# Scoring two pages of cached keys in one set of matmuls

## The chip, the cores and the metric

One core of one Trainium2 chip runs the whole program in a single launch. The metric is device time in microseconds (us), the median of several executions. The profile describes one further execution of the same program: its span is the time from its first instruction to its last, and its rows give start and duration of each instruction on five engines, TensorE (PE in the profile, its weight loads PEld), VectorE (DVE), ScalarE (ACT), GpSimd (POOL) and SyncE (SP), together with DMA transfers and the clock that TensorE was granted, as a share of its full speed (1.00).

## The reference

The program is one inference step of a one-layer decoder: a mixer that joins differential attention and a convolution branch, then cross-attention, then a feed-forward block, for a prompt of 1024 tokens and for 8 decode sequences of 4 new tokens each. All numbers are f32. The part that matters here is the differential attention of the decode sequences over cached keys that lie in pages:

```
k_past = cache_k[l, page_table].reshape(dec_b, past, N_ATT_HEADS, ATT_V_DIM)
q2 = q.reshape(B, T, H, 2, DIFF_HEAD_DIM)
s_past = einsum('bqhjd,bkhjd->bjhqk', q2, k_past.reshape(B, P, H, 2, DIFF_HEAD_DIM))
w = diff_weights(concat([s_past, s_new]), bias, lam)   # softmax1 - lam * softmax2
```

Each of the 8 sequences has 16 pages of 128 past tokens, with 4 heads of 128 channels. So there are 128 pages of 128x512 numbers (256 KB each), and for each page and head a product of 8 query rows (4 tokens, two maps) with 128 keys. The prompt's own causal differential attention is computed with the same formula in 32 steps, one for each head (4) and block of 128 queries (8).

## The kernel before

The kernel is written with an instruction list for each engine and semaphores between them, and nothing is reordered: what stands first on an engine runs first there. After the input projection comes an attention stage. It is a loop of 32 **slots**, numbered from 0 here, one for each head and query block of the prompt, the longest block (8 key blocks) first in every head and the shortest last. `attend` (line 2192) is TensorE's part of a slot: it issues the prompt's scores (`scores`, line 2039, the matmuls of line 2053), and then, for the previous slot, the turning of its weights (`turn_weights`, line 2057, in one group of up to four blocks, or in two groups when the previous slot had five blocks or more) and its product with the values (`values`, line 2071). Between these it calls `page(0)` to `page(7)`, so that every slot also carries eight pages of the decode sequences. In slots 0 to 15 these are the 128 key pages, in slots 16 to 31 the 128 value pages. Two key pages out of eight stand directly behind each other only at some places: nothing stands between pages 0 and 1, 3 and 4, 6 and 7 of most slots, the first group of turned weights stands between 1 and 2, the second group between 2 and 3, the values between 4 and 5.

The path of a key page n through slots 0 to 15:

- SyncE loads it from the cache into one of 16 page buffers (`PG`, line 556), as soon as page n-16 has been turned. A load reads its page number from `PT` first.
- TensorE turns its four heads into one of two PSUM banks, 6 and 7 (`turn_keys`, line 2079, four transposes recorded at line 1813, the line of the helper `turn`). It waits for page n-2 to have left that bank.
- ScalarE copies the bank to SBUF (`key_taken`, line 852, recorded at line 733), into `KTS[n % 3]`.
- TensorE multiplies the queries with it (`page_scores`, line 2089, matmuls of line 2099). `key_page(n)` turns page n and then scores page n-2, so the copy has the time of one page. Each of the four heads has its own 32 output rows of PSUM bank 5, and the queries, padded with zeros, are the stationary operand with 32 columns; the 128 turned keys are the moving operand. One f32 product of the program shows as two matmul records and two weight loads in the profile; a transpose shows as one of each.
- After 16 pages the bank holds a sequence's scores, four pages a row group, and VectorE copies it out (`scores_out`, line 1485). The first score of the next sequence waits for that copy (`s_taken`).

In the same slots VectorE adds the prompt's bias (L1333), takes maxima (L1335, L1337), does one tap of the convolution in most slots (four pairs of L1310 and L1313), and ends the slot with a reciprocal and the weights (L1342, L1345, L1348), for which it waits for the two exponentials of ScalarE (line 832). `turn_weights` waits for the weights. ScalarE's list has the eight copies of the key pages of a slot with the copies of turned weights, the two exponentials and the scaling of the previous slot's output (L733 with `QK`, L849) between them, in a fixed order. The first exponential stands behind the copy of the slot's page 3, the scaling behind that of page 4, the second exponential behind that of page 5.

Of the kernel before, what the change touches and what calls it, by code (L numbers as in the profile page):

```python
# [20 lines left out]
F32 = mybir.dt.float32  # L21
F32R = mybir.dt.float32r
I32 = mybir.dt.int32
# [5 lines left out]
P = 128  # L29
# [3 lines left out]
TS = DB * DS  # L33
# [6 lines left out]
PAGES = 16  # L40
# [59 lines left out]
def hymba_step(nc, io):  # L100
    ctx = ExitStack()
    with ctx:
        def sem(name):
            return ctx.enter_context(nc.semaphore(name))
# [4 lines left out]
        R1, R2A, R2B, R3 = base, base + 2 * XB, base + 3 * XB, base + 4 * XB  # L109
        RW = R3 + XB  # L110
        RC = RW + 32768
        TB4 = T * 4

        def at(name, shape, dt, off):
            return nc.alloc_sbuf_tensor_at(name, shape, dt, offset=off)
# [53 lines left out]
        GP = at("GP", [P, CT, CK - 1 + TP], F32, R2B)  # L169
        GS = at("GS", [P, CT, DB, CK - 1 + DS], F32, R2B + 16864)  # L170
        ST = [at(f"ST{i}", [P, T], F32, R2B + 21216 + TB4 * i) for i in range(2)]
        KNEW = at("KNEW", [TS, 512], F32, R2B + 21216 + 2 * TB4)
        VNEW = at("VNEW", [TS, 512], F32, R2B + 21216 + 2 * TB4 + 2048)
        VTOK = at("VTOK", [P, QT, 512], F32, R3)
        CY = at("CY", [P, CT, T], F32, R3 + 16384)
        PT = at("PT", [P, P], I32, R2B + 21216 + 2 * TB4)[64:65, :]
        OTHER = at("OTHER", [TS, DB], F32, RC + 1824 + 352)
        VS = at("VS", [P, NH, TS], F32, R3 + 33280)
        DEC = at("DEC", [P, NH, TS], F32, R3 + 33280)
# [3 lines left out]
        SD = at("SD", [P, 2, PAGES * P], F32, R1 + 32768)  # L183
        CNEW = at("CNEW", [P, CT, TS], F32, R1 + 36864)
        CTOK = at("CTOK", [TS, 2, 512], F32, R1 + 32768)
        KTS = [at(f"KTS{i}", [P, 512], F32, R1 + (49152, 51200, 65536)[i]) for i in range(3)]
        CYS = at("CYS", [TS, 512], F32, R1 + 49152)
        OB = at("OB", [P, 512], F32, R1 + 51200)
        PB = [at("PB0", [P, 2, TP], F32, R1 + 53248), at("PB1", [P, 2, TP], F32, R2B + 21216)]
# [1 line left out]
        QZB = at("QZB", [P, 2 * QG], F32, RW + 8192)  # L191
# [22 lines left out]
        PS = ctx.enter_context(nc.psum_tensor("PS", [P, 8, 512], F32))  # L214
# [39 lines left out]
        KV = 2 * QT  # L254
# [140 lines left out]
        k_taken = sem("k_taken")  # L395
# [85 lines left out]
        def _(sp):  # L481
# [37 lines left out]
            def load(dst, src, s=rows_in):  # L519
                sp.dma_start(dst, src).then_inc(s, 16)  # L520
# [13 lines left out]
            load(OTHER[:, :], io["other"])  # L534
            load(PT, io["page_table"].rearrange("b n -> (b n)").unsqueeze(0), pt_in)
            for a in range(2):
# [15 lines left out]
            def page_in(cache, b, j, slot):  # L552

                page = sp.value_load(PT[:, PAGES * b + j:PAGES * b + j + 1], min_val=0, max_val=n_pages - 1)
                src = cache[0].rearrange("n s h d -> n s (h d)")[ds(page, 1), :, :].rearrange("n s d -> (n s) d")
# [47 lines left out]
        def _(pool):  # L603
            def store(dst, src, s=outs):
                pool.dma_start(dst, src).then_inc(s, 16)
# [53 lines left out]
            pool.wait_ge(rows_taken, 2)  # L659
            store(io["k_sample"][0].rearrange("b t h d -> (b t) (h d)"), KNEW[:, :])  # L660
            store(io["v_sample"][0].rearrange("b t h d -> (b t) (h d)"), VNEW[:, :])
# [7 lines left out]
            for b in range(DB):  # L669
                for r in range(1, PAGES, 2):  # L670
                    if b:
                        pool.wait_ge(v_used, PAGES * (b - 1) + r + 1)
                    else:
                        pool.wait_ge(k_turned, PAGES * (DB - 1) + r + 1)
                    page = pool.value_load(PT[:, PAGES * b + r:PAGES * b + r + 1], min_val=0, max_val=n_pages - 1)
                    src = io["cache_v"][0].rearrange("n s h d -> n s (h d)")[ds(page, 1), :, :]
# [54 lines left out]
        def _(act):  # L731
            def copy(dst, src, **kw):
                return act.activation(dst, src, ACT.Copy, **kw)  # L733
# [68 lines left out]
            with act.Fori(0, NH // 2) as i:  # L802
                for s in range(2):
                    t = 8 + 2 * i + s
# [8 lines left out]
            with act.Fori(0, NH // 2) as i:  # L813
                for s in range(2):
                    t = 12 + 2 * i + s
# [35 lines left out]

            def key_taken(n):
                act.wait_ge(k_turned, n + 1)
                copy(KTS[n % 3][:, :], PS[:, 6 + n % 2, :]).then_inc(k_taken, 1)

            def new_rows_in(i):

                if i == 0:
                    act.wait_ge(rows_turned, 1)
                    copy(KNEW[:, :], PS[0:TS, 4, :]).then_inc(rows_taken, 1)  # L860
                if i == 1:
# [29 lines left out]
            for s, (h, qb) in enumerate(ORDER[:KV]):  # L891
                last = ORDER[s - 1] if s else None
                n = 8 * s
                key_taken(n)
                if s == 0:
                    new_rows_in(0)
                key_taken(n + 1)
                if s == 0:
                    new_rows_in(1)
                if last:  # L900
                    weights_taken(*last, 0)
                key_taken(n + 2)
                if s == 0:
                    new_rows_in(2)
                if last and len(groups(last[1])) > 1:
                    weights_taken(*last, 1)
                key_taken(n + 3)
                if s == 0:
                    new_rows_in(3)
                att_exp(h, qb, 0)  # L910
                key_taken(n + 4)
                if last:
                    att_take(*last)
                key_taken(n + 5)
                att_exp(h, qb, 1)
                softmax_step(s)
                key_taken(n + 6)
                key_taken(n + 7)
# [131 lines left out]
            for s in range(3 * KT):  # L1050
                t = TILE0["out"] + KT + s
# [756 lines left out]
        def _(pe):  # L1808
            pe.sem_inc(tile_done, AHEAD)

            def turn(dst, src):
                k = src.shape[0]
                return pe.transpose(dst, src, IDENT[0:k, 0:k])  # L1813
# [148 lines left out]
            for a in range(2):  # L1962
                x = pe.matmul(PS[:, a, :], ONES[0:1, :], GROW[:, 512 * a:512 * a + 512], start=True, stop=True)
# [24 lines left out]
            with pe.Fori(0, NH) as i:  # L1988
                for u in range(2):
# [3 lines left out]
                    for b in range(QT):  # L1993
                        x = turn(PS[:, 6 + b // 4, P * (b % 4):P * (b % 4) + P], ST[u][:, P * b:P * b + P])
# [84 lines left out]
            def turn_keys(n):  # L2079

                r = n % PAGES
                pe.wait_ge(pg_in[r // 2], 32 * (n // PAGES) + 32)
                if n >= 2:
                    pe.wait_ge(k_taken, n - 1)
                for h in range(NH):
                    x = turn(PS[:, 6 + n % 2, P * h:P * h + P], PG[:, r, P * h:P * h + P])
                x.then_inc(k_turned, 1)

            def page_scores(n):

                g, b4, j4 = n // (4 * PAGES), n % PAGES // 4, n % 4
                pe.wait_ge(k_taken, n + 1)
                if n == 0:
                    pe.wait_ge(qb_ok, 2 * NH)
                if n % PAGES == 0 and n:
                    pe.wait_ge(s_taken, n // PAGES)
                for h in range(NH):
                    own = QG * g + P * b4 + 32 * h
                    x = pe.matmul(PS[32 * h:32 * h + 32, 5, P * j4:P * j4 + P], QZB[:, own:own + 32],  # L2099
                                  KTS[n % 3][:, P * h:P * h + P], start=(n % PAGES == 0), stop=(n % PAGES == PAGES - 1),  # L2100
                                  skip_group_check=True)
                if n % PAGES == PAGES - 1:
                    x.then_inc(s_done, 1)

            def key_page(n):
                turn_keys(n)
                if n >= 2:
                    page_scores(n - 2)

            def turn_probs(g, c):  # L2110

# [132 lines left out]

            for s in range(KV):
                attend(s, lambda t: key_page(8 * s + t))
            for n in (8 * KV - 2, 8 * KV - 1):
                page_scores(n)
            for s in range(KV, NH * QT):
                attend(s, lambda t: value_page(8 * (s - KV) + t))  # L2250
            turn_weights(NH - 1, 0, 0)
# [3 lines left out]
            for h in range(NH):  # L2255
                x = pe.matmul(PS[:, 5, 0:SC].rearrange("p (g b h r) -> p g b h r", g=2, b=4, h=NH)[:, :, :, h, :],
                              VNEW[:, P * h:P * h + P],
                              SNEW[:, :].rearrange("p (g h b r) -> p g h b r", g=2, h=NH, b=4)[:, :, h, :, :],
                              start=True, stop=True)
# [20 lines left out]
            def part(k, c, first, last):  # L2280
                cols = slice(CHUNK * c, CHUNK * c + CHUNK)
                out = PS[:, c, 0:CHUNK]
                pe.matmul(out, WH[0][:, k, :], XH[:, k, cols], start=first, stop=False)
                pe.matmul(out, WH[0][:, k, :], XL[:, k, cols], start=False, stop=False)
                return pe.matmul(out, WL[0][:, k, :], XH[:, k, cols], start=False, stop=last)
# [23 lines left out]
            for c in (2, 3):  # L2309
                arrived(NH + 3 + c)  # L2310
                for n in range(2):
                    x = part(NH + c, n, False, c == 3)
# [123 lines left out]
            for q in range(QT + 1):  # L2436
# [12 lines left out]
                if q == QT:  # L2449
                    pe.wait_ge(xsm_v, 7)  # L2450
                    for a in range(2):
                        x = turn(PS[:, 2, P * a:P * a + P], OX[:, P * a:P * a + P])
# [8 lines left out]
                if q == 4:  # L2461
                    pe.wait_ge(xsm_v, 4)
                    for a in range(2):
                        x = turn(PS[:, 2, P * a:P * a + P], XS[:, P * a:P * a + P])
# [17 lines left out]
            def gate_step(u, c, k):  # L2482
                cols = slice(CHUNK * c, CHUNK * c + CHUNK)
                out = PS[:, 3 * u + c, 0:CHUNK]
                pe.matmul(out, WH[u][:, k, :], XH[:, k, cols], start=(k == 0), stop=False)
                pe.matmul(out, WH[u][:, k, :], XL[:, k, cols], start=False, stop=False)
                return pe.matmul(out, WL[u][:, k, :], XH[:, k, cols], start=False, stop=(k == KT - 1))
# [20 lines left out]
            for k in range(KT):  # L2508
                input_of("ffn", 1)(k)
                x = gate_step(0, 2, k)  # L2510
# [3 lines left out]
            for k in range(KT):  # L2514
                x = gate_step(1, 2, k)
# [77 lines left out]
```

## Time and profile before

| | us |
|---|---|
| runs of the kernel before | 1914.32, 1904.26, 1913.89 (median 1913.89) |
| profiled execution, time | 1911.54 |
| its span | 1910.0 |
| TensorE busy in the span | 1799.2 (94%) |
| VectorE, ScalarE busy | 940.7 (49%), 548.6 (29%) |
| transposes of key pages (L1813 with PG), busy | 82.0 |
| page scores (L2099), busy | 54.5 |
| copies of turned pages (L733 with KTS), busy | 75.7 |

The first page is turned at 283.9 us and the prompt's scores of slot 16 begin at 462.6 us, so the key pages take a tenth of the span. Busy is the union of the instructions' times on an engine. Matmuls overlap each other, so their mean duration (286 ns for a page score) is far more than the time that each adds; the start of the next work on the engine tells what a set of them costs.

### The profile page before, as it was taken

The page shows a single profiled execution, that of the slowest core. Times are in us where ns is not written, and L with a number is a line of the kernel's source. Part 1 is how long each engine was busy: PE and PEld are TensorE (multiplying, and loading weights), DVE is VectorE, ACT ScalarE, POOL GpSimd, SP SyncE. Part 2 cuts the span into 40 slices and gives each one's busy share as a digit, 9 for nine tenths or more (in the row PEclk, how much of TensorE's full clock was granted, in tenths as well). Part 3 has the DMA queues.
Part 4 walks back from the last instruction along what each step waited for, and adds up shares of the span by engine and source line. Part 5 has one row for each costly group of instructions (what it writes and reads, how often), then busy time and mean ns, then how long its engine had stood idle before and what let it go on. Part 6 is the DMA issues. An engine that isn't in the chain of part 4 may idle for free.

```text
span 1910.0 us, 33059 instructions
## 1 busy us (share of the span) xinstructions
PE 1799.2 (94%) x13461; PEld 1657.0 (87%) x13461; DVE 940.7 (49%) x1245; ACT 548.6 (29%) x993; POOL 91.6 (5%) x138
## 2 busy tenths in 40 slices
PE   7999998999988988998999899999999999999996
PEld 6999985665557978996789789999999999999995
DVE  6328887886665466222353753333233332233456
ACT  6202116676565255103432531110001000010133
POOL 2100010001320000001000000000000000000001
PEclk9999999999998999999999999999999999999997
DMA  5422127766884223234402331111112111111322
GB/s 173 137 71 77 55 69 223 226 186 199 286 284 182 67 89 133 89 110 155 150 30 80 94 114 44 44 44 45 44 54 56 45 44 45 44 44 38 134 74 91
DMA packets 149374, 199.06 MB, mean 104 GB/s; under 512 B 8105, under 2 KB 110715, under 8 KB 148872
## 3 DMA queue, kind: packets, MB, share of 16 engines
q1 hardware_dynamic: 134318, 133.00, 22.8%
q0 software_dynamic: 14944, 64.53, 9.6%
q8 instruction: 76, 1.25, 0.3%
q14 instruction: 34, 0.28, 0.0%
q10 hardware_dynamic: 2, 0.00, 0.0%
HBM read 177.19 MB, written 20.74 MB: 104 GB/s over the span
## 4 chain that ended last, share of the span: by engine, by line
PE 53%; DVE 5%; ACT 2%; issue 2%; POOLq 0%; POOL 0%; DVEq 0%; ACTq 0%
PE PS L1823 15%; PE PS L1824 15%; PE PS L1825 15%; PE PS L1813 2%; PE PS L2376 2%; PE PS L2397 1%; DVE WL L1550 1%; ACT WH L733 1%; PE PS L1837 1%; PE PS L1838 1%; PE PS L1839 1%; PE PS L1862 1%; DVE H L1580 1%; DVE Y L1577 1%; DVE HST L1778 0%
## 5 line engine op out<-in xcount | busy, mean ns | idle before, releaser
L1823 PE MATMUL PS<-XH,WH 128*128 128x352 f32 x1984 | 645.0, 325 | 7.7 <-DVE WL L1550 5.7
L1824 PE MATMUL PS<-XL,WH 128*128 128x352 f32 x1984 | 638.1, 322 | 0.0
L1825 PE MATMUL PS<-XH,WL 128*128 128x352 f32 x1984 | 637.6, 321 | 0.0
L1196 DVE CAST WH<-RAW 128x1024 fp32r<-128x1024 f32 x112 | 78.8, 704 | 634.2 <-PE PS L1825 614.0
L1823 PEld LDWEIGHTS PS<-XH,WH 128*128 128x128 f32 x1984 | 374.1, 189 | 9.6 <-DVE WL L1550 6.5
L1824 PEld LDWEIGHTS PS<-XL,WH 128*128 128x128 f32 x1984 | 374.7, 189 | 0.0
L1825 PEld LDWEIGHTS PS<-XH,WL 128*128 128x128 f32 x1984 | 373.6, 188 | 0.0
L1310 DVE SCALAR_TENSOR_TENSOR CY<-GP,DW,CY 128x1024 f32<-128x1024 f32 x124 | 158.5, 1278 | 1.0 <-DVE CY L1313 1.0
L1823 PE MATMUL PS<-HH,WH 128*128 128x352 f32 x468 | 154.0, 329 | 2.9 <-DVE Y L1769 2.7
L1824 PE MATMUL PS<-HL,WH 128*128 128x352 f32 x468 | 152.4, 326 | 0.0
L1825 PE MATMUL PS<-HH,WL 128*128 128x352 f32 x468 | 152.2, 325 | 0.0
L1198 DVE TENSOR_TENSOR WL<-RAW,WH 128x1024 fp32r<-128x1024 f32 x112 | 137.3, 1226 | 3.8
L1142 ACT ACTIVATE TA<-TA 128x1056 f32<-128x1056 f32 x22 | 23.9, 1087 | 364.9 <-DVE TA L1730 364.9
L733 ACT ACTIVATE HH<-TA 128x1056 f32 x22 | 23.9, 1086 | 251.9 <-DVE TA L1736 251.9
L1823 PEld LDWEIGHTS PS<-HH,WH 128*128 128x128 f32 x468 | 89.9, 192 | 3.7 <-DVE WL L1550 3.2
L1824 PEld LDWEIGHTS PS<-HL,WH 128*128 128x128 f32 x468 | 90.0, 192 | 0.0
L1825 PEld LDWEIGHTS PS<-HH,WL 128*128 128x128 f32 x468 | 89.7, 192 | 0.0
L1813 PE MATMUL PS<-IDENT,PG 128*128 128x128 f32 x512 | 82.0, 283 | 5.2 <-DMA PG<-in_cache_k 2.6
L733 ACT ACTIVATE KTS<-PS 128x512 f32<-128x512 f32 x128 | 75.7, 601 | 35.7 <-PE PS L1813 35.3
L1813 PEld LDWEIGHTS PS<-IDENT,PG 128*128 128x128 f32 x512 | 56.7, 142 | 25.5 <-issue 21.3
L1550 DVE TENSOR_TENSOR WL<-RAW,WH 128x1024 fp32r<-128x1024 f32 x38 | 46.5, 1223 | 58.7 <-ACT WH L733 58.7
L2099 PE MATMUL PS<-KTS,QZB 128*32 128x128 f32 x1024 | 54.5, 286 | 2.2 <-DVE SD L1485 2.0
(342 smaller groups left out, 2303.5 us busy)
## 6 DMA issues: line engine op xcount, KB each, us to landing
PG<-in_cache_k SPq DMA_DIRECT2D x128, 256.0 KB, 3.0
PG<-in_cache_v SPq DMA_DIRECT2D x64, 256.0 KB, 4.3
PG<-in_cache_v POOLq DMA_DIRECT2D x64, 256.0 KB, 4.4
RAW<-in_w_gate SPq DMA_DIRECT2D x22, 512.0 KB, 4.1
RAW<-in_w_up SPq DMA_DIRECT2D x22, 512.0 KB, 5.2
RAW<-in_w_in SPq DMA_DIRECT2D x20, 512.0 KB, 6.4
RAW<-in_w_out SPq DMA_DIRECT2D x16, 512.0 KB, 4.5
RAW<-in_w_xo SPq DMA_DIRECT2D x16, 512.0 KB, 4.3
```

The costliest lines, as they stand in the source:

```text
L733: return act.activation(dst, src, ACT.Copy, **kw)
L1142: act.activation(TA[:, :], TA[:, :], ACT.Silu).then_inc(silu_ok, 1)
L1196: dve.tensor_copy(WH[v % 2][:, :, :], raw).then_inc(hi_done, 1)
L1198: dve.tensor_tensor(WL[v % 2][:, :, :], raw, WH[v % 2][:, :, :].bitcast(F32), ALU.subtract)\
L1310: dve.scalar_tensor_tensor(out=CY[:, c, 0:TP], in0=GP[:, c, ds(j, TP)], scalar=w, in1=CY[:, c, 0:TP], op0=ALU.mult, op1=ALU.add).then_inc( ...
L1550: dve.tensor_tensor(WL[t % 2][:, :, :], RAW[t // 2 % 2][:, :, P * (t % 2):P * (t % 2) + P], WH[t % 2][:, :, :].bitcast(F32), ALU.subtract) ...
L1813: return pe.transpose(dst, src, IDENT[0:k, 0:k])
L1823: pe.matmul(out, WH[u][:, k, :], xh[:, k, cols], start=(k == 0), stop=False)
L1824: pe.matmul(out, WH[u][:, k, :], xl[:, k, cols], start=False, stop=False)
L1825: mm = pe.matmul(out, WL[u][:, k, :], xh[:, k, cols], start=False, stop=(k == kt - 1))
L2099: x = pe.matmul(PS[32 * h:32 * h + 32, 5, P * j4:P * j4 + P], QZB[:, own:own + 32], KTS[n % 3][:, P * h:P * h + P], start=(n % PAGES == 0) ...
L2376: x = pe.matmul(PSF[:, NMEM * h:NMEM * h + NMEM], Y[:, 2 * h + k, P * q:P * q + P], KMT[:, 2 * h + k, :], start=(k == 0), stop=(k == 1))
```

## The change

Key pages are scored in pairs. A key page is still turned and copied by itself, but on even pages `key_page` now only turns. On an odd page n it turns, and then `pair_scores(n - 3)` scores pages n-3 and n-2 with one set of matmuls, in which the moving operand has 256 columns: 128 of the first page and 128 of the second. The products, their sums and the bank they go to stay as they were; there are 256 products of the program instead of 512. The pair waits for both copies, and the wait for VectorE's copy of the previous sequence moves with the pair.

A pair needs its two turned pages in one tile, so three buffers `KTS[n % 3]` become two tiles of two pages each. The second page of the second tile lies where `KNEW` and the page table `PT` were, and these two move; they keep their size. The second tile's two pages are 65,504 bytes apart in each partition, the first tile's 2,048 bytes.

```diff
-        KNEW = at("KNEW", [TS, 512], F32, R2B + 21216 + 2 * TB4)
+        KNEW = at("KNEW", [TS, 512], F32, R1 + 40960)
...
-        PT = at("PT", [P, P], I32, R2B + 21216 + 2 * TB4)[64:65, :]
+        PT = at("PT", [P, P], I32, R2B + 21216 + 2 * TB4 + 2048)[64:65, :]
...
-        KTS = [at(f"KTS{i}", [P, 512], F32, R1 + (49152, 51200, 65536)[i]) for i in range(3)]
+        KTS_AT = (49152, 51200, 65536, R2B - R1 + 21216 + 2 * TB4)
+        KTS = [at(f"KTS{i}", [P, 2, (KTS_AT[2 * i + 1] - KTS_AT[2 * i]) // 4], F32, R1 + KTS_AT[2 * i]) for i in range(2)]
...
             def key_taken(n):
                 act.wait_ge(k_turned, n + 1)
-                copy(KTS[n % 3][:, :], PS[:, 6 + n % 2, :]).then_inc(k_taken, 1)
+                copy(KTS[n // 2 % 2][:, n % 2, 0:512], PS[:, 6 + n % 2, :]).then_inc(k_taken, 1)
...
-            def page_scores(n):
+            def pair_scores(n):
 
                 g, b4, j4 = n // (4 * PAGES), n % PAGES // 4, n % 4
-                pe.wait_ge(k_taken, n + 1)
+                pe.wait_ge(k_taken, n + 2)
                 if n == 0:
                     pe.wait_ge(qb_ok, 2 * NH)
                 if n % PAGES == 0 and n:
                     pe.wait_ge(s_taken, n // PAGES)
                 for h in range(NH):
                     own = QG * g + P * b4 + 32 * h
-                    x = pe.matmul(PS[32 * h:32 * h + 32, 5, P * j4:P * j4 + P], QZB[:, own:own + 32],
-                                  KTS[n % 3][:, P * h:P * h + P], start=(n % PAGES == 0), stop=(n % PAGES == PAGES - 1),
-                                  skip_group_check=True)
-                if n % PAGES == PAGES - 1:
+                    x = pe.matmul(PS[32 * h:32 * h + 32, 5, P * j4:P * j4 + 2 * P].rearrange("p (a t) -> p a t", a=2),
+                                  QZB[:, own:own + 32], KTS[n // 2 % 2][:, :, P * h:P * h + P],
+                                  start=(n % PAGES == 0), stop=(n % PAGES == PAGES - 2), skip_group_check=True)
+                if n % PAGES == PAGES - 2:
                     x.then_inc(s_done, 1)
 
             def key_page(n):
                 turn_keys(n)
-                if n >= 2:
-                    page_scores(n - 2)
+                if n % 2 and n >= 3:
+                    pair_scores(n - 3)
...
             for s in range(KV):
                 attend(s, lambda t: key_page(8 * s + t))
-            for n in (8 * KV - 2, 8 * KV - 1):
-                page_scores(n)
+            pair_scores(8 * KV - 2)
```

## Rows read from the trace of the kernel before

**Rows 1.** Busy time by window: stretch, us, PE, PEld, DVE, ACT, POOL, PEclk, DMA, GB/s.
```profile
285.00:465.00 180.00, 169.70 (x1886) 110.65 (x1887) 140.26 (x243) 121.82 (x273) 8.39 (x16) 0.99 0.71 210
...
356.20:365.50 9.30, 9.30 (x115) 6.00 (x111) 8.44 (x16) 6.54 (x17) 0.00 (x0) 1.00 0.80 229
```

**Rows 2.** Groups by form, 285 to 465 us: busy, mean ns, idle before and releaser.
```profile
L733 ACT ACTIVATE KTS<-PS 128x512 f32<-128x512 f32 x128 | 75.7, 601 | 35.7 <-PE PS L1813 35.3
...
L2099 PE MATMUL PS<-KTS,QZB 128*32 128x128 f32 x1024 | 54.5, 286 | 2.2 <-DVE SD L1485 2.0
```

**Rows 3.** Waits, 285 to 465 us: who waited for whom, total us, times, longest.
```profile
DVE SMALL L1342 <- ACT PB L832: 24.4, 13, 6.1
...
PEld PS L2099 <- ACT KTS L733: 7.9, 37, 1.6
...
PE PS L1813 <- ACT KTS L733: 2.6, 2, 1.6
...
PE PS L2099 <- DVE SD L1485: 2.0, 2, 1.4
...
PE PS L1813 <- DVE SNEW L1407: 1.1, 1, 1.1
```

**Rows 4.** Timeline of PE in slot 5: start, us, instruction; turns and scores alternate.
```profile
350.20 0.42 PE L2099 MATMUL PS<-KTS,QZB 128*32 128x128 f32 x8
350.56 0.66 PE L1813 MATMUL PS<-IDENT,PG 128*128 128x128 f32 x4
351.14 0.43 PE L2099 MATMUL PS<-KTS,QZB 128*32 128x128 f32 x8
351.50 0.65 PE L1813 MATMUL PS<-IDENT,PG 128*128 128x128 f32 x4
```

**Rows 5.** Timeline, slots 4 and 5: turns behind full-width work, and the second group of weights.
```profile
338.97 0.66 PE L1813 MATMUL PS<-IDENT,PB 128*128 128x128 f32 x4
...
339.47 0.60 PE L1813 MATMUL PS<-IDENT,PG 128*128 128x128 f32 x4
339.67 0.60 ACT L733 ACTIVATE WT<-PS 128x512 f32<-128x512 f32 x1 [0.34 <-PE PS L1813]
...
340.46 0.33 PE L1813 MATMUL PS<-IDENT,PB 128*128 128x128 f32 x1
...
353.44 0.60 PE L1813 MATMUL PS<-IDENT,PG 128*128 128x128 f32 x4
353.97 0.42 PE L2099 MATMUL PS<-KTS,QZB 128*32 128x128 f32 x8
```

**Rows 6.** Timeline of PE: prompt scores with 256 and with 128 moving columns, and what follows.
```profile
356.21 0.70 PE L2053 MATMUL PS<-QK 64*128 64x256 f32 x4
356.84 0.66 PE L1813 MATMUL PS<-IDENT,PG 128*128 128x128 f32 x4
...
365.48 0.49 PE L2053 MATMUL PS<-QK 64*128 64x128 f32 x4
365.91 0.66 PE L1813 MATMUL PS<-IDENT,PG 128*128 128x128 f32 x4
```

**Rows 7.** By form and timeline: the scores of the new tokens, a moving operand in pieces.
```profile
L2027 PE MATMUL PS<-QZB,QK 128*32 128x64 f32 x8 | 0.6, 219 | 0.0
...
291.54 0.61 PE L2027 MATMUL PS<-QZB,QK 128*32 128x64 f32 x8
```

**Rows 8.** Timeline of PE: the first turned weights of slot 1.
```profile
303.22 0.92 PE L1813 MATMUL PS<-IDENT,PB 128*128 128x128 f32 x4 [2.67 <-issue]
```

**Rows 9.** Timeline of SP in slot 5, and the page's DMA issues (KB each, us to landing).
```profile
349.80 12.40 SPq L556 DMA_DIRECT2D PG<-in_cache_k  x11
...
PG<-in_cache_k SPq DMA_DIRECT2D x128, 256.0 KB, 3.0
```

**Rows 10.** Timeline: VectorE's weights of slot 6, and TensorE's turn of them in slot 7.
```profile
365.36 0.48 DVE L1348 SCALAR_TENSOR_TENSOR PB<-PB,SMALL 128x256 f32<-128x256 f32 x1
...
367.79 0.44 PE L1813 MATMUL PS<-IDENT,PB 128*128 128x128 f32 x2
```

## The prediction

> **What bounds the kernel now.** I read the busy time of the stage first. From 285 to 465 us TensorE is busy 169.70 of 180 us, VectorE 140.26, ScalarE 121.82 [rows 1]. So TensorE sets the pace, but VectorE stands close behind: in slot 6 it is busy 8.44 of 9.30 us [rows 1]. The waits come next, to see how often TensorE is held up. What they name is small: 7.9 and 2.6 us for ScalarE's copies of turned pages, 2.0 us for VectorE's copy of a sequence's scores, 1.1 us for its copy behind SNEW [rows 3], and once 2.67 us for the first turned weights [rows 8]. The other side waits longer: VectorE waits 24.4 us in 13 places for the exponentials [rows 3], and ScalarE 35.7 us for turned pages [rows 2]. An edit that shortens TensorE's list therefore shortens the stage, until VectorE's spare time is used up. Third, the timeline of TensorE, because busy time hides what matters: the score records have a mean of 286 ns, yet 1024 of them take 54.5 us together [rows 2]. Only the distance from one start to the next shows what a set costs.
>
> **The change part by part: the sets.** A page's scores start at 350.20, its successor's turns at 350.56, the next scores at 351.14 [rows 4]. So a set of scores costs 0.36 us, a set of four turns behind it 0.58, and a page 0.94; two pages cost 1.88.
>
> After the change a pair is turns, turns, one wide set. Turns that follow full-width work are cheaper than turns that follow a score: from 353.44 to 353.97 is 0.53 us [rows 5], and four turns followed by four more take 339.47 - 338.97 = 0.50 [rows 5]. Two blocks of turns then cost 0.50 + 0.53 = 1.03. This holds wherever the page stands, since turned weights and values, the work between pages, are full-width too.
>
> The wide set isn't in the trace. Below, it costs 0.36, as if the columns were free; above, 2 x 0.36 = 0.72, as if nothing were shared. The nearest rows are the prompt's scores, also two f32 products side by side in a part of the array: with 128 columns such a set takes 365.91 - 365.48 = 0.43 us, with 256 it takes 356.84 - 356.21 = 0.63 [rows 6]. So 0.21 us of the set scales with 128 columns and the rest is paid once per set. I take 0.36 + 0.21 = 0.57.
>
> A pair then costs 1.03 + 0.57 = 1.60 instead of 1.88, a gain of 0.28, and 64 pairs gain 18 us. By the bounds of the wide set the gain is 0.13 to 0.49 a pair, 8 to 31 us. The part that goes isn't the multiplying, it is the passage from transposes to scores and back.
>
> **What of it stays.** From the 18 us I take what is caught by waits.
>
> Slots 0 and 1: the first weights at 303.22 wait 2.67 us for VectorE's chain [rows 8], which has work of its own for the new tokens. What TensorE gains before that (five pairs, 1.4 us) only lengthens that wait, except some 0.25 us by which ScalarE reaches the first exponential sooner. Loss 1.15.
>
> Slots 1 to 4 and 9 to 12 turn weights in two groups through the same bank, and the second waits for ScalarE's copy of the first. Today the scores of page 2 lie in between and hide it. The copy starts 0.70 us after the first group and takes 0.60, so the second group can't start before about 1.34; it started at 340.46, 1.49 behind 338.97 [rows 5]. After the change only a block of turns is between, ready at about 0.94. The new wait is 0.40; eight of them would be 3.2 us, of which I count 2.9, as the first falls in a delayed stretch.
>
> Waits that move: the wait of 2.0 us, in two places, is for the copy of the previous sequence's scores [rows 3]. The pair asks for it one page later. In slot 2 I expect it gone, a gain of 0.6; in slot 8 VectorE's chain is longer and the wait stays, but page 3's turns are then done before it, so the slot keeps its gain.
>
> VectorE and ScalarE: in slot 12 the turn of the decode weights waits 1.1 us for VectorE's copy behind SNEW [rows 3], and that copy stands after a convolution tap, so what TensorE gains earlier in the slot is lost: 0.45. The 2.6 us in which turns wait for copies are two waits, 1.6 in slot 0 and the other 1.0 at the start of slot 10 [rows 3]; there the copy stands behind ScalarE's decode exponential, so the 0.28 that TensorE gains after slot 9's second exponential is lost.
>
> Elsewhere the spare time suffices. In the slots from 5 to 7 TensorE gains 4 x 0.28 = 1.1 us each, and VectorE has 9.30 - 8.44 = 0.86 spare [rows 1], so it falls behind by about 0.3 us a slot, some 0.9 by slot 7. There it can afford more: its weights of slot 6 are done at 365.84 and turned at 367.79, 1.95 us later [rows 10]. Slot 8 has no convolution tap and it catches up.
>
> SyncE issues page loads 12.40/11 = 1.1 us apart and a load lands in 3.0 us [rows 9]. Eight pages are 9.0 us, more than the new slots 6 and 7 (9.3 - 1.1 = 8.2 us), but loads run up to 16 pages ahead, and over the 16 slots TensorE still needs more than 1.2 us a page. So this costs nothing; without the lead, a page of slots 5 to 8 would arrive about 1 us late in every slot. The move of KNEW and PT changes no instruction.
>
> The sum: 18.2 - 1.15 - 2.9 + 0.6 - 0.45 - 0.28 = 14.0 us. Behind slot 15 the same chain starts 14 us earlier, and nothing there hangs on an absolute time. The profiled execution took 1911.5 us (span 1910.0), so 1897.5. It lies 2.4 us under the median of the runs shown, which is 1913.9; profile and runs average 1911.0, so I take the profiled one as typical and predict 1898.
>
> **The rivals.** *All of it stays* (0.13): the second group's wait falls beside other delays and VectorE keeps up. Then 1911.5 - 18 = 1893.5. For it speaks VectorE's 24.4 us of waiting [rows 3], against it that this is spread unevenly (slot 15 alone has 6.1).
>
> *ScalarE's copies become the wait* (0.17). Two turned pages in a row fill both banks. A copy starts 0.70 us after the first turn of its block [rows 5] and takes 0.60 [rows 2]; the second of two starts when the first is done, so it ends at 0.70 + 1.20 = 1.90 after the pair's first turn. Its bank is wanted again after the pair and one more block of turns, at 1.60 + 0.50 = 2.10. That leaves 0.2. Between some copies stand exponentials and the output's scaling. If 0.3 us were missing at two places in each slot, 32 x 0.3 = 9.6 us would go and the gain shrink to 4: 1907. Against it: ScalarE waits 35.7 us for turned pages today [rows 2] and is busy 6.54 us of a slot of 9.30 [rows 1]. The Trainium skill, TensorEngine Tiling (Array Packing), section PSUM Bottleneck, warns of this case: splitting the array speeds up TensorE but not the copies out of PSUM, which may become the bottleneck. By that rule this rival would be the result; the trace has the copies at 75.7 us in a stage of 180 [rows 2].
>
> *The wide set costs nearly two narrow ones* (0.05), so that only the saved passage between turns remains: 8 us less the same losses of about 4, again 1907.
>
> *Slower* (0.06): the moving operand now comes in two pieces, in every second pair 65,504 bytes apart. If its second piece were streamed slowly, a wide set could exceed two narrow ones. To end 0.5% slower than before (1923.5) each pair must lose (14 + 9.6)/64 = 0.37 us, so the wide set must take 0.94 instead of 0.57; it decides from 0.79, where the gain of 14 is gone. Against it: eight score matmuls with 64 columns in pieces of 8 take 0.61 us in all, of which the last one's own 0.22, so 0.06 each [rows 7], no slower per column than the rest.
>
> **How the numbers follow.** The forecast, 10 to 17 us saved, has 0.59; the rivals 0.13, 0.17, 0.05 and 0.06. About 0.5%, 9.6 us, is what a measurement of this kernel can tell from no change. Faster by more takes the forecast and the first rival: 0.72. Within it fall the second and third: 0.22. Slower: 0.06. The forecast's own range is 1893 to 1904. The range to hold eight times in ten reaches from 1890 (the full gain, and 3 us for the difference between executions) to 1908 (the second and third rival).
>
> **What would show it.** In the profile after: 512 score records of 256 columns in place of 1024; a pair's period near 1.60 us where no wait is in it; 0.57 us from a wide set to the next turns; a wait of about 0.4 us of L1813 with PB for ScalarE's WT in slots 2 to 4 and 9 to 12; VectorE's waiting at L1342 much smaller than 24.4 us; slot 16 beginning near 448.6 instead of 462.6. The prediction is wrong if waits of L1813 with PG for KTS grow past 5 us, if 0.57 is nearer 0.72, or if slot 16 begins 14 us earlier and the end doesn't.

## The result, and the profile after

| | before | after |
|---|---|---|
| median of the runs, us | 1912.24 (8 runs, 1904.12 to 1914.32) | 1897.88 (8 runs, 1894.95 to 1900.11) |
| profiled execution, us | 1911.54 | 1897.24 |
| its span, us | 1910.0 | 1895.7 |

The ratio is 0.9926, with a 95% interval of 0.9915 to 0.9937: 14 us, or 0.7%, faster. The forecast was 1898.0. In the changed kernel all lines named here stand one lower (turns L1814, copies L734, scores L2100).

First the busy time by window (columns as in [rows 1]), of the key pages' stage and of the new slot 6, which now takes 8.00 us instead of 9.30.

```profile
285.00:451.00 166.00, 153.56 (x1395) 101.36 (x1393) 140.82 (x245) 119.03 (x273) 8.49 (x16) 0.99 0.75 228
350.60:358.60 8.00, 8.00 (x82) 5.35 (x78) 7.87 (x13) 6.41 (x17) 0.00 (x0) 1.00 0.79 242
```

TensorE's busy time in the stage fell by 16.1 us; VectorE's and ScalarE's busy times are nearly as before, in a shorter stage. In slot 6 VectorE is now busy 7.87 of 8.00 us: its idle time, 0.86 us of the slot before, has shrunk to 0.13. Next the groups by form of the same stage, beside [rows 2].

```profile
L734 ACT ACTIVATE KTS<-PS 128x512 f32<-128x512 f32 x128 | 72.4, 600 | 26.4 <-PE PS L1814 26.1
...
L2100 PE MATMUL PS<-KTS,QZB 128*32 128x256 f32 x512 | 40.9, 391 | 1.5 <-DVE SD L1486 1.3 <-ACT KTS L734 0.2
```

There are 512 records of 256 columns, and they are busy 40.9 us where 1024 narrow ones took 54.5. Then the waits of 285 to 451 us, beside [rows 3].

```profile
DVE SMALL L1343 <- ACT PB L833: 13.9, 6, 4.7
...
PEld PS L1814 <- ACT WT L734: 3.7, 8, 0.5
PE PS L1814 <- ACT KTS L734: 3.0, 2, 1.9
PEld PS L2100 <- ACT KTS L734: 2.7, 5, 1.5
...
PE PS L1814 <- ACT WT L734: 1.8, 7, 0.3
...
PE PS L1814 <- DVE SNEW L1408: 1.5, 1, 1.5
...
PE PS L2100 <- DVE SD L1486: 1.3, 1, 1.3
```

VectorE waits in 6 places instead of 13. TensorE's matmuls have one new wait, for WT, in seven places (slots 2 to 4 and 9 to 12): the second group of turned weights waits for ScalarE's copy of the first. The weight loads (PEld) show it in eight places, with slot 1; before, they had waited for WT in six places, 1.2 us in all, and the matmuls in none. Of the two waits for the scores' copy (SD) one is left, and the one behind SNEW grew from 1.1 to 1.5. Last the timeline of TensorE in slot 4, beside [rows 4, 5].

```profile
334.57 0.64 PE L2100 MATMUL PS<-KTS,QZB 128*32 128x256 f32 x8
335.14 0.66 PE L1814 MATMUL PS<-IDENT,PB 128*128 128x128 f32 x4
335.63 0.60 PE L1814 MATMUL PS<-IDENT,PG 128*128 128x128 f32 x4
336.49 0.33 PE L1814 MATMUL PS<-IDENT,PB 128*128 128x128 f32 x1 [0.25 <-ACT WT L734]
...
339.89 0.64 PE L2100 MATMUL PS<-KTS,QZB 128*32 128x256 f32 x8
340.46 1.09 PE L1814 MATMUL PS<-IDENT,PG 128*128 128x128 f32 x8
341.48 0.64 PE L2100 MATMUL PS<-KTS,QZB 128*32 128x256 f32 x8
```

A wide set costs 340.46 - 339.89 = 0.57 us, the two blocks of turns behind it 341.48 - 340.46 = 1.02, so a pair 1.59 instead of 1.88. The second group of weights starts 336.49 - 335.14 = 1.35 behind the first, and its row shows 0.25 of idle time. Before, it started 1.49 behind [rows 5], with the scores of a page in between.

Where the gain comes from is read from the first record of the prompt's scores in each slot (start of L2053 before, L2054 after):

| slot | before, us | after, us | earlier by | gained in the slot |
|---|---|---|---|---|
| 0 | 280.07 | 280.15 | -0.08 | 0.95 |
| 1 | 295.61 | 294.74 | 0.87 | 0.54 |
| 2 | 313.11 | 311.70 | 1.41 | 1.38 |
| 3 | 325.16 | 322.37 | 2.79 | 0.75 |
| 4 | 336.03 | 332.49 | 3.54 | 0.86 |
| 5 to 8 | 346.45 | 342.05 | 4.40 | 1.21, 1.27, 1.20, 1.24 |
| 9 | 385.63 | 376.31 | 9.32 | 0.74 |
| 10 | 397.58 | 387.52 | 10.06 | 0.63 |
| 11 | 410.01 | 399.32 | 10.69 | 0.74 |
| 12 | 420.87 | 409.44 | 11.43 | 0.30 |
| 13 to 15 | 432.86 | 421.13 | 11.73 | 1.20, 1.29, 1.10 |
| 16 | 462.63 | 447.31 | 15.32 | |

The gain is spread over the slots: about 1.2 us (four pairs of 0.30) where nothing interferes, 0.63 to 0.86 where weights are turned in two groups, 0.30 where the wait behind SNEW takes more. Slots 0 and 1 differ from execution to execution, so their gain is less sure than that of slots 2 to 15 (the last experiment has numbers). From slot 16 to the end 1.0 us is lost again; the last experiment bears on that too.

### The profile page after: what moved, and what is told of

Read it like the earlier page. It is cut to its first block, busy times and chain, and to the rows that moved or that the text cites. A ratio compares the mean times of both kernels' runs of the same rounds, so it can differ in the third digit from the quotient of the medians.

```text
span 1895.7 us, 32035 instructions
## 1 busy us (share of the span) xinstructions
PE 1785.1 (94%) x12949; PEld 1649.9 (87%) x12949; DVE 940.2 (50%) x1245; ACT 546.3 (29%) x993; POOL 92.1 (5%) x138
## 3 DMA queue, kind: packets, MB, share of 16 engines
q8 instruction: 72, 1.18, 0.3%
## 4 chain that ended last, share of the span: by engine, by line
PE 54%; DVE 5%; ACT 2%; issue 2%; POOLq 0%; POOL 0%; DVEq 0%; ACTq 0%
PE PS L1824 15%; PE PS L1825 15%; PE PS L1826 15%; PE PS L1814 2%; PE PS L2376 2%; PE PS L2397 1%; DVE WL L1551 1%; ACT WH L734 1%; PE PS L1838 1%; PE PS L1840 1%; PE PS L1839 1%; PE PS L1863 1%; DVE H L1581 1%; DVE Y L1578 1%; DVE HST L1779 0%
## 5 line engine op out<-in xcount | busy, mean ns | idle before, releaser
L734 ACT ACTIVATE HH<-TA 128x1056 f32 x22 | 23.9, 1088 | 251.9 <-DVE TA L1737 251.9
L734 ACT ACTIVATE KTS<-PS 128x512 f32<-128x512 f32 x128 | 72.4, 600 | 26.4 <-PE PS L1814 26.1
L1814 PE MATMUL PS<-IDENT,PG 128*128 128x128 f32 x512 | 74.2, 280 | 5.1 <-ACT KTS L734 3.0
L1814 PEld LDWEIGHTS PS<-IDENT,PG 128*128 128x128 f32 x512 | 57.3, 142 | 23.8 <-issue 19.9
L833 ACT ACTIVATE PB<-PS,SMALL 128x1024 f32<-128x1024 f32 (+7 forms) x64 | 47.7, 745 | 2.1 <-DVE SMALL L1338 2.0
```

Source lines behind the costliest of these rows:

```text
L833: act.activation(PB[r][:, m, 0:n], PSF[:, TP * m:TP * m + n], ACT.Exp, bias=NMX2[r][:, m:m + 1], scale=SCALE, accum_out=SUM2[r][:, m:m + 1 ...
```

## The experiments

The theory is the forecast's: the time lies in the passages between turns and scores, the new wait is the second group's, and TensorE still sets the pace. The rivals are that the wide set itself saves time, that the buffers do, and that VectorE or ScalarE limits the gain.

**Narrow sets in the order of the change.** Order and buffers are those of the change; only the pair is scored by two sets of 128 columns, one directly behind the other.

```diff
-                for h in range(NH):
-                    own = QG * g + P * b4 + 32 * h
-                    x = pe.matmul(PS[32 * h:32 * h + 32, 5, P * j4:P * j4 + 2 * P].rearrange("p (a t) -> p a t", a=2),
-                                  QZB[:, own:own + 32], KTS[n // 2 % 2][:, :, P * h:P * h + P],
...
+                for a in range(2):
+                    for h in range(NH):
+                        own = QG * g + P * b4 + 32 * h
+                        x = pe.matmul(PS[32 * h:32 * h + 32, 5, P * (j4 + a):P * (j4 + a) + P], QZB[:, own:own + 32],
+                                      KTS[n // 2 % 2][:, a, P * h:P * h + P], start=(n % PAGES + a == 0),
...
```

> The order, the waits and the buffers of the change stay, but a pair is scored by two sets of 128 columns, one behind the other, in place of one set of 256. Theory: most of the gain is the saved passage from transposes to scores and back, and little comes from the width. Three narrow sets that stood behind each other at the end of the key pages before the change began 0.24 us apart, and the wide set adds 0.21 us for its second page, so a pair should cost 0.03 us more than after the change: 64 x 0.03 = 2 us slower than the change, still 12 us faster than before. Rival, the width makes the gain (a set pays its fixed part again each time): a second set costs 0.36, a pair 0.15 us more, 10 us slower than the change, 5 us faster than before.

Measured: 1896.96 us (median of 6, 1894.55 to 1897.71), ratio to before 0.9921 (0.9905 to 0.9937). The interval covers that of the change. The timeline of TensorE in slot 4:

```profile
339.82 0.65 PE L2101 MATMUL PS<-KTS,QZB 128*32 128x128 f32 x16
340.40 1.09 PE L1814 MATMUL PS<-IDENT,PG 128*128 128x128 f32 x8
341.42 0.65 PE L2101 MATMUL PS<-KTS,QZB 128*32 128x128 f32 x16
```

Two narrow sets take 0.58 us together, one wide set 0.57. Between the starts of slots 2 and 16 this kernel needs 135.84 us, the change 135.61: the 256 columns are worth 0.23 us over 56 pairs, where 0.03 a pair, 1.7 us, had been expected. The loads of the stationary operand doubled (1024 records, busy 24.3 us instead of 10.1) and cost no more than that on the path. The row behind the 0.24 of the expectation stood in the trace of before: at the end of the key pages one narrow set begins at 461.52 and the next at 461.76. The third begins only at 462.28, behind a wait.

**The buffers of the change in the order of before.** The other half of that pair of kernels: two tiles of two pages, moved KNEW and PT, but each page is scored by itself behind the next but one's turns.

```diff
-                pe.wait_ge(k_taken, n + 2)
+                pe.wait_ge(k_taken, n + 1)
...
-                                  QZB[:, own:own + 32], KTS[n // 2 % 2][:, :, P * h:P * h + P],
...
+                    x = pe.matmul(PS[32 * h:32 * h + 32, 5, P * j4:P * j4 + P], QZB[:, own:own + 32],
+                                  KTS[n // 2 % 2][:, n % 2, P * h:P * h + P], start=(n % PAGES == 0),
...
-                if n % 2 and n >= 3:
-                    pair_scores(n - 3)
+                if n >= 2:
+                    page_scores(n - 2)
```

> The buffers of the change (four turned pages, KNEW and PT moved) with the order of before: each page's turns followed by the scores of the page two back, in sets of 128 columns. It differs from the run with narrow sets in order alone. Theory: the order is the gain, so this takes the time of before, within 1 us at slot 16, and lies 15 us behind the run with narrow sets there. Rival, the fourth buffer or the places of the buffers make part of the gain: 3 us or more faster than before.

Measured: 1910.53 us (median of 10, 1902.57 to 1913.92), ratio 0.999 (0.9972 to 1.0009): the interval holds 1, so no change is shown. Slot 16 begins at 460.94, 1.69 us earlier than before, where at most 1 was expected; but 1.68 of that is there at the start of slot 2 (311.43), and 1.08 at the start of slot 0. From slot 2 on the buffers alone give 0.01 us (149.51 us to slot 16, 149.52 before). The timeline in slot 4:

```profile
336.00 0.43 PE L2100 MATMUL PS<-KTS,QZB 128*32 128x128 f32 x8
336.35 0.66 PE L1814 MATMUL PS<-IDENT,PG 128*128 128x128 f32 x4
336.94 0.43 PE L2100 MATMUL PS<-KTS,QZB 128*32 128x128 f32 x8
```

The page costs 336.94 - 336.00 = 0.94, as before. This kernel and the one with narrow sets issue the same matmuls of the same shape on the same buffers and differ only in their order, and in the wait for the copies that goes with it; between slots 2 and 16 they need 149.51 and 135.84 us. So 13.67 of the 13.91 us that the change gains there are order: two blocks of turns and two sets of scores in a row instead of one and one. The difference lies in both: two sets fall from 2 x 0.35 = 0.70 to 0.58, two blocks of turns from 2 x 0.59 = 1.18 to 1.02. The Trainium skill, TensorEngine Tiling (Array Packing), section Key Properties, says that a change of the tiling mode drains TensorE. These rows agree in the sense that each pair with one passage to the 32-column scores and back instead of two is 1.88 - 1.60 = 0.28 us shorter; that the drain is the cause they don't show.

**A lighter VectorE.** In slots 1 to 15 two of the four channel groups of a convolution tap work on 64 columns instead of 1024. A part of the convolution is left out.

```diff
+                    m = 64 if light and c >= 2 else TP
-                    dve.scalar_tensor_tensor(out=CY[:, c, 0:TP], in0=GP[:, c, ds(j, TP)], scalar=w,
-                                             in1=CY[:, c, 0:TP], op0=ALU.mult, op1=ALU.add).then_inc(conv_step, 1)
+                    dve.scalar_tensor_tensor(out=CY[:, c, 0:m], in0=GP[:, c, ds(j, m)], scalar=w,
+                                             in1=CY[:, c, 0:m], op0=ALU.mult, op1=ALU.add).then_inc(conv_step, 1)
...
-                    conv(tap)
+                    conv(tap, True)
```

> The change, with VectorE's convolution tap in slots 1 to 15 cut to 64 of 1024 columns for two of the four channel groups (that part of the convolution is left out), about 2.3 us less of VectorE's work in a slot. Theory: TensorE sets the pace and VectorE's lag is affordable, so slot 16 begins earlier by only some 1.5 to 2 us, the wait behind SNEW in slot 12 that the tap causes. Rival, VectorE became the second bound after the change: slot 16 begins 5 us or more earlier, with gains in slots 5 to 7, 10 and 11.

Measured, in one execution: 1896.84 us; slot 16 begins 1.87 us earlier than after the change (445.44), as expected. The waits of 285 to 450 us show that VectorE really became free:

```profile
DVE SMALL L1344 <- ACT PB L833: 34.7, 16, 5.3
```

It now waits for the exponentials in 16 places, and yet TensorE starts slot 12 only 0.29 us earlier. The other 1.59 us come in slot 12 alone, where the wait behind SNEW is gone. So VectorE, busy 7.87 of 8.00 us in slot 6, does not set the pace of the plain slots; it costs time in one place, where a copy for TensorE stands behind a tap.

**The second group of weights later.** In slots that turn weights in two groups, page 3 is turned first, then the second group, then the pair is scored; ScalarE takes page 3 before the second group's copy.

```diff
+                key_taken(n + 3)
                 if last and len(groups(last[1])) > 1:
                     weights_taken(*last, 1)
...
-                key_taken(n + 3)
...
-                if last and len(groups(last[1])) > 1:
-                    turn_weights(*last, 1)
-                page(3)
+                two = last and len(groups(last[1])) > 1
+                if two and s < KV:
+                    turn_keys(8 * s + 3)
+                    turn_weights(*last, 1)
+                    pair_scores(8 * s)
+                else:
+                    if two:
+                        turn_weights(*last, 1)
+                    page(3)
```

> The change, with the second group of turned weights moved behind the turns of page 3 and ahead of the scores (ScalarE's copies in the same order). Theory: the wait of 0.25 us in seven slots for ScalarE's copy of the first group goes and comes back nowhere, 1.8 us faster than the change, 16 us faster than before. Rival: it turns into a wait of the values for the second group's copy, and the time stays that of the change.

Measured: 1892.73 us (median of 6, 1889.52 to 1896.36), ratio 0.9907 (0.9891 to 0.9924). The timeline of TensorE in slot 4:

```profile
332.22 0.66 PE L1814 MATMUL PS<-IDENT,PB 128*128 128x128 f32 x4
332.71 1.04 PE L1814 MATMUL PS<-IDENT,PG 128*128 128x128 f32 x8
333.58 0.31 PE L1814 MATMUL PS<-IDENT,PB 128*128 128x128 f32 x1
333.82 0.42 PE L2100 MATMUL PS<-KTS,QZB 128*32 128x256 f32 x4
```

The second group now starts 1.36 behind the first, as after the change (1.35), but two blocks of turns lie between instead of one, and no idle time is left. These rows also show where the time of a passage lies: a block of turns with other turns on both sides takes (333.58 - 332.71)/2 = 0.435 us, one between two sets of scores 0.59. Slots 3 and 4 are each 0.43 us shorter than after the change, slots 9 to 11 0.43 to 0.44. So the new wait cost 0.43 in each of these five, close to the forecast's 0.40, and not the 0.25 that stands in the row: of a wait the row shows the time in which no matmul was running, and the tail of the matmuls before it hides the rest. The gain of 4.36 us at the start of slot 16 is not all the edit's, since slot 0 began 1.57 earlier in this execution, slot 1 0.18 later and slot 2 2.19 earlier. The edit's part is what slots 2 to 15 gave, 2.17 us, against 1.8 expected; slot 2 gave only 0.30. In slot 12 0.31 us was lost: the wait behind SNEW is 2.3 us here instead of 1.5.

**Three waits.** The same, and two more: in the long slots ScalarE's decode exponential moves behind its last page copy, and VectorE's copy behind SNEW moves ahead of the tap.

```diff
-                softmax_step(s)
+                if s % QT >= 4:
+                    softmax_step(s)
...
+                if s % QT < 4:
+                    softmax_step(s)
...
+                if g is not None and s % QT == 4 and s < KV:
+                    new_weights(g)
...
                     conv(tap)
...
```

> The same, and two more waits that the prediction counted: ScalarE's decode exponential goes behind the slot's last copies of turned pages, and VectorE's copy behind SNEW goes ahead of the convolution tap. Theory: besides the 1.8 us, the wait of 1.06 us in slot 10 and that of 1.55 us in slot 12 go, 4.4 us faster than the change, 18.7 us faster than before. Rival: VectorE or ScalarE is late elsewhere by then, and less than 2.5 us of the 4.4 arrives at slot 16.

Measured: 1892.12 us (median of 6, 1884.67 to 1892.95), ratio 0.989 (0.9871 to 0.991), the fastest of all kernels here, though its interval overlaps that of the kernel before it. Slot 16 begins 6.19 us earlier than after the change (441.12), of which 1.53 is there at the start of slot 2; slots 2 to 15 gave 4.66, against 4.4 expected. Slot 10 gave 1.45 of it (0.44 is the second group's wait) and slot 12 1.43: the waits for the copy behind the decode exponential and behind SNEW are gone. In their place TensorE now waits for VectorE, 0.20 us for weights and 0.52 us for the scores' copy, which the change had not had in slots 11 and 12:

```profile
397.87 0.66 PE L1819 MATMUL PS<-IDENT,PB 128*128 128x128 f32 x4 [0.20 <-DVE PB L1352]
...
409.63 0.64 PE L2105 MATMUL PS<-KTS,QZB 128*32 128x256 f32 x8 [0.52 <-DVE SD L1491]
```

So the next waits to come up are for VectorE, in slots 11 and 12 first.

**Short copies.** From page 4 on ScalarE copies 256 of a turned page's 512 columns; the scores of two heads then use old keys.

```diff
-                copy(KTS[n // 2 % 2][:, n % 2, 0:512], PS[:, 6 + n % 2, :]).then_inc(k_taken, 1)
+                m = 512 if n < 4 else 256
+                copy(KTS[n // 2 % 2][:, n % 2, 0:m], PS[:, 6 + n % 2, 0:m]).then_inc(k_taken, 1)
```

> The change, with ScalarE's copies of turned pages cut from 512 to 256 columns from page 4 on (the keys of two heads are then old ones), which takes about 0.2 us from each copy. Theory: ScalarE has the 0.2 us to spare that the prediction found, so slot 16 begins at most 1 us earlier, from the wait in slot 10; the wait for the copy of turned weights doesn't hang on these copies. Rival, the copies became the wait: slot 16 begins 4 us or more earlier.

Measured, in one execution: 1895.83 us. The groups by form and the busy time of 285 to 451 us:

```profile
L734 ACT ACTIVATE KTS<-PS 128x256 f32<-128x256 f32 x124 | 46.9, 386 | 31.8 <-PE PS L1815 29.9
```

```profile
285.00:451.00 166.00, 152.44 (x1390) 101.00 (x1390) 141.91 (x246) 96.23 (x270) 7.65 (x15) 0.99 0.77 229
```

A copy takes 386 ns instead of 600 and ScalarE is busy 96 instead of 119 us. The lead over the change is 1.84 us at the start of slot 2 already (1.47 of it from ahead of slot 0) and still 1.86 at slot 8. Only in slots 8 (0.25), 10 (0.47) and 15 (0.32) does it grow, to 2.91 at slot 16, where at most 1 was expected. So at the full pace of slots 2 to 7 shorter copies gain nothing; all that they gain between slots 2 and 16 is 1.07 us.

**The kernel before once more.** No edit; for the clock behind slot 15.

> The kernel before once more, to see how its granted clock falls around slot 16 in another execution. After the change the clock was at 0.5 for 6.8 us there, and 1.8 of the 15.3 us gained at slot 16 were given back; before, it stayed at 1.00. Theory: TensorE waits 2.6 us there in both kernels, and whether the clock falls differs from execution to execution. Rival: the change brings it, and this run stays at 1.00 in slot 16.

Measured: 1912.54 us, span 1911.0. It reaches slot 16 at 462.61, within 0.02 us of the first execution. The slots from 2 to 15 repeat themselves (149.51 us, 149.52 in the first), but slots 0 and 1 don't: they took 34.31 us at a mean granted clock of 0.85, in the first execution 33.04 at 0.95. Here is what comes next, the busy time by window in the first execution of the kernel before, in this second one and after the change, each from some 5.5 us behind the start of slot 16.

```profile
468.00:475.00 7.00, 5.53 (x83) 3.27 (x83) 5.40 (x10) 4.05 (x10) 1.61 (x3) 1.00 0.65 203
```

```profile
468.00:475.00 7.00, 5.96 (x65) 3.72 (x67) 4.59 (x9) 4.16 (x10) 1.45 (x3) 0.76 0.50 150
```

```profile
453.00:460.00 7.00, 6.69 (x63) 3.98 (x65) 4.46 (x9) 4.27 (x10) 1.08 (x2) 0.52 0.54 150
```

The granted clock was 1.00 in the first execution, 0.76 on average in the second, 0.52 after the change. In all three TensorE has just been idle for 2.6 us there, waiting for VectorE's copy of the last sequence's scores (SD). So a stretch at the lower level, 1.2 GHz, occurs in the kernel before too, though not in each execution. Against the first execution the change loses 15.32 - 13.68 = 1.64 us in slot 16; against the second only 0.72 (15.30 - 14.58), and at the end its span is 1911.0 - 1895.7 = 15.3 us shorter, as much as at the start of slot 16. The other five kernels with the order of the change had the same wait and averaged 0.76 over the same 7 us, and so did the one with the buffers alone. So 0.52 is the exception among nine traces, and none of them shows that the change brings the lower clock: with the order of before it came in two executions of three, with that of the change in six of six, which is too few to tell how likely it is in either.

## Why the prediction was right

The forecast was a sum, 14.0 us, and 14.3 came out. Its parts:

| step of the forecast | forecast, us | measured, us |
|---|---|---|
| a wide set | 0.57 | 0.57 |
| a pair | 1.60 | 1.59 |
| gain of a slot without waits | 4 x 0.28 = 1.12 | 1.10 to 1.29 |
| wait of the second group | 0.40 | 0.43 in five slots (by what its removal gives) |
| wait for scores in slot 2 gone | 0.6 | 1.38 gained in that slot, 0.63 more than in slot 3 |
| slot 10, with the decode exponential | 1.12 - 0.40 - 0.28 = 0.44 | 0.63 |
| slot 12, behind SNEW | 1.12 - 0.40 - 0.45 = 0.27 | 0.30 |
| slot 16 earlier by | 14.0 | 15.3 |
| end earlier by | 14.0 | 14.3 |

**The passage, not the multiplying.** Right, and more so than the working had it. The forecast gave 0.15 us of a pair's gain to the wide set (0.72 to 0.57) and 0.13 to the turns (1.16 to 1.03). The kernel with narrow sets has both without a wide set. The upper bound, 2 x 0.36, was the step that was wrong: it took each narrow set with its own passage, as it stands today, also where two follow each other. Two in a row cost 0.58. The row that speaks against it, 0.24 us from one narrow set to the next, was in the trace of before and was overlooked. One reading was off without harm: the turns of 0.50 us [rows 5] don't stand behind full-width work but behind a set of scores (which starts at 338.62), with turns following. A pair has one block of that kind and one of the other, so the 1.03 held, at 1.02. For the reason of the two sets in a row the third rival, a wide set at the price of two narrow ones, gave no 1907: it is nearly what happens, and it costs nothing.

**What stays.** The new wait stands in the seven places that were named for it, slots 2 to 4 and 9 to 12, and costs within 0.03 us what was forecast in the five slots in which that can be read (3, 4, 9, 10 and 11). Slots 8 and 12 went as forecast, slot 10 gained 0.63 instead of 0.44. Two terms were sized a little low: slots 0 and 1 gained 1.49 us together, against 8 x 0.28 - 1.15 - 0.1 = 1.0 (0.1 is what was counted of slot 1's wait for the second group), and the free slots gained 1.10 to 1.29 instead of 1.12. The two make up most of the 1.3 us by which slot 16 begins earlier than forecast. The first of them isn't sure: against the second execution of the kernel before, slots 0 and 1 gained 2.76 us. The sum also has 18.2 where 64 x 0.28 is 17.9. It came out at the end all the same, because the stretch behind slot 16 ran at the lower clock after the change and not in the execution that the sum was made against. That the end agrees to 0.3 us is luck: the gain up to slot 16 was forecast 1.3 us too small, and 1.0 us was lost behind it. That "nothing there hangs on an absolute time" isn't contradicted; that two executions differ by about a microsecond there was not in it.

**VectorE.** It falls behind as forecast and can nearly everywhere afford it; slot 12 is the place where it can't. The weights of slot 6 are written from 359.45 to 359.94 us and turned at 360.61, 0.67 later, where 1.95 stood before [rows 10]; it fell behind by 1.28, a little more than the forecast's 0.9. At slot 8, which has no tap, VectorE waits 1.02 us for the prompt's scores again. Its waits for the exponentials fell from 24.4 to 13.9 us; they were forecast to become "much smaller" than 24.4, and that is only half right.

**The rivals.** All of the 18 us staying: the seven waits of the second group (some 7 x 0.43 = 3.0 us) and those of slots 0, 1, 10 and 12 took more than the difference, and the wait for scores that went in slot 2 gave some back. ScalarE's copies as the wait: of the 9.6 us that it would have cost, the kernel with short copies finds 1.07, and none in slots 2 to 7. The Trainium skill, TensorEngine Tiling (Array Packing), section PSUM Bottleneck, says that the copies out of PSUM may become the bottleneck; here they did not, at 72.4 us of copies in a stage of 166. The moving operand in two pieces: eight records in a row take 0.57 us (339.89 to 340.46) in the timeline, and the next pair, which is in the other tile, 0.57 as well (341.48, followed at 342.05 by the prompt's scores), so 65,504 bytes between the pieces cost nothing that these rows show.

## What to carry to other kernels

Where TensorE alternates between full-width work and work in narrow column groups, count the passages: grouping two blocks of the same kind saved 0.28 us a pair here, and making the matmuls wider added nothing to that. Price an operation from the rows where it stands behind its own kind, not only where it stands today. And when a block between two dependent steps is taken away, look at what it was hiding: here 0.43 us was given back in each of five slots, which moving one block of turns into the gap recovers.

## What the hardware showed that was not expected

Eight f32 score products with 128 columns (16 records) take 0.58 us, four with 256 columns (8 records) 0.57: the second narrow set costs 0.58 - 0.35 = 0.23 us behind the first, with all its weight loads. An idle time of 0.25 us shown before a matmul cost the path 0.43, since the modelled end of the work before it covers the rest. And in the same place of the same program, behind an idle time of 2.6 us, the granted clock stayed at 1.00 in one execution and averaged 0.76 over 7 us in another.
